# Attention products with 64 rows padded to 128 rows in a one-core transformer layer in fp32

## What is computed

```python
def diff_attention(q, k, v, ...):            # branch A, 4 heads with 2 maps each
    ...
        s = jnp.einsum('bqhmd,bkhmd->bhmqk', q[:, q0:k_len], k[:, :k_len]) * scale
        s = jnp.where(allowed, s + bias[None, :, None], NEG_INF)
        p = jax.nn.softmax(s, axis=-1)
        w = p[:, :, 0] - lam * p[:, :, 1]
        outs.append(jnp.einsum('bhqk,bkhe->bqhe', w, v[:, :k_len]))
...
def sliding_window_sink_attention(...):      # branch B, 8 heads on 2 heads of k and v;
    ...                                      # a chunk of 64 queries sees 2 chunks of 64 keys
def chunk_band_attention(...):               # branch C, 8 heads, all earlier chunks
```

## Time and profile before

| | before |
|---|---|
| median of 3 runs | 924.96 us (924.56 to 925.87) |
| profiled execution, first to last instruction | 925.7 us |
| PE busy | 900.7 us, 97% |
| DVE, ACT, POOL busy | 453.8, 396.4, 369.5 us |
| share of PE in the chain that ended last | 86% |
| attention slots in the trace | from about 39 us to about 353 us |

### The profile page before, as it was taken

One profiled execution on the slowest core, in us unless ns is written; L12 is line 12 of the kernel. 1 busy time (PEld: TensorE's weight loads), 2 busy tenths in 40 slices (PEclk: granted clock), 3 DMA queues, 4 the chain that ended last, 5 costly groups with the idle time before them and its releaser, 6 DMA issues.

```text
span 925.7 us, 12765 instructions
## 1 busy us (share of the span) xinstructions
PE 900.7 (97%) x4327; PEld 742.3 (80%) x4327; DVE 453.8 (49%) x887; ACT 396.4 (43%) x700; POOL 369.5 (40%) x195
## 2 busy tenths in 40 slices
PE   7999999999999999999999999999999999999997
PEld 6877777877787778788888779888888888888886
DVE  4677786665566562353334155655555555400004
ACT  4455445566555563434333144534443444312112
POOL 4333223322222332754455454544444444444441
PEclk9999999999999999999999999999999999999999
DMA  7431133221222210433333721433333332323202
GB/s 226 128 112 45 46 90 91 72 73 59 63 63 75 74 58 24 137 101 92 90 92 113 241 77 47 137 91 91 106 97 91 92 107 95 113 102 103 91 23 92
DMA packets 132140, 86.13 MB, mean 93 GB/s; under 512 B 6822, under 2 KB 121454, under 8 KB 132098
## 3 DMA queue, kind: packets, MB, share of 16 engines
q1 hardware_dynamic: 131050, 81.86, 29.5%
q10 hardware_dynamic: 1048, 3.72, 1.2%
HBM read 83.42 MB, written 2.14 MB: 92 GB/s over the span
## 4 chain that ended last, share of the span: by engine, by line
PE 86%; DVE 8%; ACT 2%; issue 2%; DMA 1%; POOL 0%; ACTq 0%; DVEq 0%; SPq 0%; POOLq 0%
PE banks L1220 26%; PE banks L1222 26%; PE banks L1221 26%; PE banks L1363 3%; PE banks L1295 2%; PE banks L1294 2%; DVE lam_ratio L1045 1%; DMA wide<-in_g_pre_mix_dram 1%; PE banks L1239 1%; DVE pages L942 1%; ACT pages L657 1%; DVE scratch L878 1%; DVE pages L937 1%; DVE scratch L1020 1%; ACT pages L623 0%
## 5 line engine op out<-in xcount | busy, mean ns | idle before, releaser
L518 POOL TENSOR_TENSOR ring_lo<-ring_raw,ring_hi 128x1024 fp32r<-128x1024 f32 x142 | 343.8, 2423 | 499.0 <-ACT ring_hi L615 498.8
L1220 PE MATMUL banks<-u_hi,ring_hi 128*128 128x512 f32 (+1 forms) x800 | 310.3, 388 | 0.0
L1222 PE MATMUL banks<-u_hi,ring_lo 128*128 128x512 f32 (+1 forms) x800 | 305.6, 382 | 0.0
L1221 PE MATMUL banks<-u_lo,ring_hi 128*128 128x512 f32 (+1 forms) x800 | 305.1, 381 | 0.0
L615 ACT CAST ring_hi<-ring_raw 128x1024 fp32r<-128x1024 f32 x142 | 147.7, 1043 | 133.4 <-PE banks L1222 125.3
L1222 PEld LDWEIGHTS banks<-u_hi,ring_lo 128*128 128x128 f32 x800 | 150.7, 188 | 29.5
L1220 PEld LDWEIGHTS banks<-u_hi,ring_hi 128*128 128x128 f32 x800 | 151.0, 189 | 27.5 <-DVE u_lo L884 0.2
L1221 PEld LDWEIGHTS banks<-u_lo,ring_hi 128*128 128x128 f32 x800 | 151.0, 189 | 27.5
L1185 DVE SCALAR_TENSOR_TENSOR wide<-banks,cols,wide 128x511 f32<-128x511 f32 x88 | 65.9, 749 | 87.4 <-ACT wide L837 80.6
L1220 PE MATMUL banks<-ring_hi,pages 128*128 128x512 f32 x240 | 93.8, 391 | 1.7 <-DVE scratch L1118 1.6
L1221 PE MATMUL banks<-ring_lo,pages 128*128 128x512 f32 x240 | 93.4, 389 | 0.0
(11 more groups left out here) (134 smaller groups left out, 1051.1 us busy)
## 6 DMA issues: line engine op xcount, KB each, us to landing
ring_raw<-in_w_ffn_up_dram SPq DMA_DIRECT2D x88, 256.0 KB, 3.1
ring_raw<-in_w_in_dram SPq DMA_DIRECT2D x60, 256.0 KB, 3.3
ring_raw<-in_w_gate_dram SPq DMA_DIRECT2D x48, 256.0 KB, 3.1
ring_raw<-in_w_ffn_down_dram SPq DMA_DIRECT2D x44, 256.0 KB, 2.7
ring_raw<-in_w_out_dram SPq DMA_DIRECT2D x16, 256.0 KB, 2.9
scratch<-in_x_dram SPq DMA_DIRECT2D x4, 512.0 KB, 6.5
ring_raw<-in_w_proj_a_dram SPq DMA_DIRECT2D x8, 256.0 KB, 2.7
ring_raw<-in_w_proj_c_dram SPq DMA_DIRECT2D x8, 256.0 KB, 3.0
```

What stands on the lines that cost most here:

```text
L518: pool.tensor_tensor(wlo[:, r, :], raw[:, r, :], whi[:, r, :].bitcast(F32), ALU.subtract).then_inc(w_lo_done, 1)
L1220: pe.matmul(out, lhs_hi, rhs_hi, start=start, stop=False)
L1221: pe.matmul(out, lhs_hi, rhs_lo, start=False, stop=False)
L1222: return pe.matmul(out, lhs_lo, rhs_hi, start=False, stop=stop)
```

## The change

Three places are changed.

The low part of q gets a page for each map (`q_lo_page(u, m)`), in which the rows of the other map are zero, and L1295 reads all 128 rows of q and of k. DVE clears the four half pages at the start of the program, and `qk(0)` waits for it. The number of products stays.

In B the two blocks of keys change places (the whole tile first), and `pv` reads all 128 rows of the half tile's block: the rows 0 to 63 of its probabilities are zero. POOL clears them once, in slot 33, after `pv(31)`; `pv(33)` waits for it.

`turn_probs` takes its columns accordingly. ACT and DVE copy the two blocks in the new order, with the same shapes.

```diff
+Q_LO_PG = Y_HI + 10
...
-    return qt * P - CHUNK, [(qt - 1, CHUNK, CHUNK), (qt, 0, P)]
+    return qt * P - CHUNK, [(qt, 0, P), (qt - 1, CHUNK, CHUNK)]
...
-        def q_lo_page(u):
-            return QK_PG + 5 * (u % 2) + 2
+        def q_lo_page(u, m):
+
+            return QK_PG + 5 * (u % 2) + 2 if m == 0 else Q_LO_PG + u % 2
...
+                if s == TT * 8 + 1:
+
+                    pool.wait_ge(pv_done, TT * 8)
+                    pool.wait_ge(w_lo_done, sum(split_slot(t) <= s for t in range(T_ATT + RING)))
+                    pool.memset(pages[0:CHUNK, PT_PG:PT_PG + 4, P:2 * P].bitcast(F32), 0.0).then_inc(probs_cleared, 1)
+                    pool.wait_ge(probs_cleared, 1)
...
+            dve.memset(pages[CHUNK:P, QK_PG + 2:QK_PG + 8:5, :].bitcast(F32), 0.0).then_inc(q_lo_cleared, 1)
+            dve.memset(pages[0:CHUNK, Q_LO_PG:Q_LO_PG + 2, :].bitcast(F32), 0.0).then_inc(q_lo_cleared, 1)
...
-                            hi, lo = pages[half_rows(m), q_page(n, m), :], pages[half_rows(m), q_lo_page(n), :]
+                            hi, lo = pages[half_rows(m), q_page(n, m), :], pages[half_rows(m), q_lo_page(n, m), :]
...
-                        rows = half_rows(m)
-                        pairs = ((pages[:, q_page(u, m), cq], pages[:, k_page(u, m), ck]),
-                                 (pages[rows, q_lo_page(u), cq], pages[rows, k_page(u, m), ck]))
+                        pairs = [(pages[:, pg, cq], pages[:, k_page(u, m), ck])
+                                 for pg in (q_page(u, m), q_lo_page(u, m))]
...
+                if s == 4 * 8 + 1:
+                    pe.wait_ge(probs_cleared, 1)
-                for b, (kt, p0, nk) in enumerate(blocks):
-                    rows = slice(p0, p0 + nk)
+                for b, (kt, _, _) in enumerate(blocks):
+
                     pc = slice(b * P, (b + 1) * P)
-                    v_hi_b, v_lo_b = (pages[rows, pg, kt * P:(kt + 1) * P] for pg in (vh, vl))
+                    v_hi_b, v_lo_b = (pages[:, pg, kt * P:(kt + 1) * P] for pg in (vh, vl))
...
-                                    v_hi_b, v_lo_b, pages[rows, PT_PG:PT_PG + 2, pc],
-                                    pages[rows, PT_PG + 2:PT_PG + 4, pc], b == 0, b == len(blocks) - 1)
+                                    v_hi_b, v_lo_b, pages[:, PT_PG:PT_PG + 2, pc],
+                                    pages[:, PT_PG + 2:PT_PG + 4, pc], b == 0, b == len(blocks) - 1)
...
-                    col = 0
-                    for b, (_, _, nk) in enumerate(blocks):
+                    for b, (kt, p0, nk) in enumerate(blocks):
+                        col = kt * P + p0 - k0
                         last = pe.transpose(psum[0:nk, PT_BANK + m, b * P:(b + 1) * P],
                                             scratch[:, P_PAGE + m, col:col + nk], ident[:])
-                        col += nk
...
+            pe.wait_ge(q_lo_cleared, 2)
             qk(0)
```

More of the change, by code:

```diff
@@ L297, in build_encoder @@
         mask_b_done = sem("mask_b_done")
+        q_lo_cleared = sem("q_lo_cleared")
+        probs_cleared = sem("probs_cleared")
         squares = sem("squares")
@@ L1328, in pv @@
                     pe.wait_ge(y_lo, y_count(u - 1, qt // 2))
-                for b, (kt, p0, nk) in enumerate(blocks):
-                    rows = slice(p0, p0 + nk)
+                if s == 4 * 8 + 1:
+                    pe.wait_ge(probs_cleared, 1)
+                for b, (kt, _, _) in enumerate(blocks):
                     pc = slice(b * P, (b + 1) * P)
-                    v_hi_b, v_lo_b = (pages[rows, pg, kt * P:(kt + 1) * P] for pg in (vh, vl))
+                    v_hi_b, v_lo_b = (pages[:, pg, kt * P:(kt + 1) * P] for pg in (vh, vl))
                     if branch(u) == "A":
                         last_b = b == len(blocks) - 1
-                        pe.matmul(psum[:, O_BANK + s % 2, 0:2 * P], pages[rows, PT_PG, pc],
-                                  pages[rows, vh:vh + 2, kt * P:(kt + 1) * P], start=b == 0, stop=False)
-                        mm = pe.matmul(psum[:, O_BANK + s % 2, 0:P], pages[rows, PT_PG + 2, pc], v_hi_b,
+                        pe.matmul(psum[:, O_BANK + s % 2, 0:2 * P], pages[:, PT_PG, pc],
+                                  pages[:, vh:vh + 2, kt * P:(kt + 1) * P], start=b == 0, stop=False)
+                        mm = pe.matmul(psum[:, O_BANK + s % 2, 0:P], pages[:, PT_PG + 2, pc], v_hi_b,
                                        start=False, stop=last_b)
@@ L1350, in turn_probs @@
                 u, qt = divmod(s, TT)
-                _, blocks = keys_of(u, qt)
+                k0, blocks = keys_of(u, qt)
                 maps = 1 if branch(u) == "A" else 2
```

## The result

The changed kernel took 914.37 us (median of 4 runs, 911.96 to 915.46) against 925.41 us of the kernel before in the same series (4 runs): a ratio of 0.9872, with a 95% interval of 0.9855 to 0.9889. So it is faster, by 11.0 us. The forecast was 907.3 with a range of 902.5 to 912.5: the direction was right, and the time lies outside the range.

What follows compares the result with a forecast made beforehand. The prediction took PE, busy for 97% of the span, as the bound: 24.9 us saved on PE, 7.2 lost in waits, 17.7 kept. 924.96 - 17.7 = 907.3 us, range 902.5 to 912.5 with half of rivals 1 and 2.

Steps and rivals of the forecast that it cites:

- The price of a passage between 64 and 128 rows: On PE, each passage between 64-row and 128-row products costs about 0.17 us; four score products hold four passages.
- Rivals 3 to 5: PE's clock falls, 931 (2%); change doesn't do what it says, 924 to 926 (1%); 64-row products already overlap, 935 (1%).
- rival 1: PE keeps everything it saves, 24.9 us, because its waits move with it: 899 to 903.5; 8%.
- the first scores: Scores ahead of the loop: 0.5 us kept.
- the slots with qt = 1: Middle slots with scores of 384 keys: 0.68 us saved and kept in each, but 0.33 in slot 1.
- the slots with qt = 0 but slot 4: First slots of units, 256-key scores: nothing kept in 0, 8, 12; 0.46 us in 16; 0.66 each in 20, 24, 28.
- the cover of the clearings: DVE's two clearings at the start, at most about 2.5 us, hide in 8.7 idle us before its load lands; nothing added.
- three signs of being wrong: The qt = 3 stretches change length, middle slots show waits, or more windows stand at half clock.
- The step that failed: Last slots of units (qt = 3): stretch keeps its length, moving with the transposes before; 4.5 us of savings there become waits.
- rival 2: Waits swallow more: DVE steps newly fall beside POOL's, each such slot giving back 0.7 us; 911 to 920; 14%.
- The base: Starting time of the forecast: runs' median of 924.96 us, taken as 0.7 below the profiled execution's span of 925.7.
- The bounds that the prediction names: One clock fall either way, 1.2 us for transposes, 0.6 for POOL, 0.02 on each of 31 savings: 903.5 to 911, 74%.

Runs made afterwards that it cites:

- back_512: The changed kernel with 64 rows again in the 512-key scores of units 1, 2, 3 and 7 alone; 912.5 us in one run.
- own_bank: The changed kernel with branch A's transposes of v and y in the PSUM bank that its probabilities don't use; 916.21 us in one run.
- pool_late: The changed kernel with POOL's low part of the weights waiting for the slot's probabilities in slots with qt = 3; 906.24 us, ratio 0.9776.
- back_pv: The changed kernel with 64 rows of the half tile again in pv(33), pv(37), pv(41) and pv(43), new block order kept; 914.5 us in one run.
- half_only: The changed kernel with only B's half tile at 128 rows and the new block order, A's and C's scores as before; 922.99 us, ratio 0.9969.

## Why the prediction was wrong

**What held.** The price of a passage between 64 and 128 rows did: 0.12 and 0.23 us a step, 0.94 for `pv`, 23.3 us off PE. Rivals 3 to 5 are out, and so is rival 1. So did the first scores, the slots with qt = 1, slots 1 and 2, the slots with qt = 0 but slot 4, the cover of the clearings, and PE's waits for L1069 (5.7 us, "about 5.6") and L1102 (3.1 us, "2 to 3"). The attention's end did not: the transposes of slot 47 start at 345.1 us in place of 358.3, so 13.2 earlier and not 18. Two of the three signs of being wrong that the prediction named did come: the slots with qt = 3 changed length (8.04 to 8.30 us in A), and the middle slots of A showed waits (for L988). With the clock alike the attention and the two `pv` behind it kept 13.6 us; the sum had 17.7.

**The step that failed** is this, under the last slots of a unit: "so the stretch keeps its length. This holds for its slow steps too [...]: POOL's work starts from ACT's, which moves with the same chain." ACT's L626 hangs on the transposes of y in the slots with qt = 2 of units 1 to 3, not on the transposes of the probabilities; POOL's L523 starts from it and holds DVE; and the sums of the pairs stay at 14.96 to 14.99 us whatever PE saves in between (`back_512`, `own_bank`). All of 3 x 0.70 = 2.1 us was counted as kept and was lost. The time of 914.4 lies in the range of rival 2 (a DVE step beside POOL takes back 0.7 us in a slot), and the mechanism is near it, but it was not in the middle slots, where that rival looked for it, and in the slots read hardly a step newly fell beside POOL (in slot 19 L1037 takes 0.27 us in place of 0.17): those that were held before are held on.

**The same mistake, smaller.**
- I had read for slots 6, 10 and 14 only that the softmax is done early, and overlooked that `turn_probs` waits there for the low part of y as well, which the kernel's text says. `own_bank` removed it and got the forecast 6.25. By itself it cost nothing, as the pair was bound anyway. In slot 18 the same wait has no such cover and is most of the 0.2 us lost in 18 + 19: the slot saved 0.57 us and not 0.70, and its transposes start at 163.71, 0.14 us after L988's end.
- Slot 31 grew from 8.31 to 8.99 us: 0.7 us lost. DVE waits 0.90 us for ACT's L710, which stands behind L681 (k of B) in ACT's queue; L960 follows late, and PE's scores wait for it:

```profile
248.89 0.33 PE L1306 MATMUL banks<-pages 128*128 128x128 f32 x1 [0.50 <-DVE pages L960]
```

  From L681's start to slot 31's transposes it takes 8.94 us in after and in before (241.06 to 250.00, and 251.85 to 260.79), whatever PE does in between. The pair of slots 30 and 31 keeps its sum too, 15.22 before, 15.18 after and 15.16 in `back_512`. POOL has no part in it: slot 31 takes 8.98 in `pool_late`. Another order of ACT's queue was not tried.
- In B 0.21 us of each `pv` ahead of a last slot, and of slot 44, comes back as a wait (`back_pv`), and the rest saved 0.35 rather than 0.4: 0.9 us in all. Slots 18 + 19 lost 0.2, and 22 + 23 and 26 + 27 together gained 0.2 more than thought.
- Slot 4: its 0.45 was read in the one execution in which the clock fell there; in others there is nothing to save.

2.1 + 0.7 + 0.9 + 0.45 make 4.15 us, and 4.1 lie between 17.7 and 13.6; what is left over are differences of 0.1 to 0.2.

**The base.** "The median of the runs lies 0.7 below that execution" had the span against a time. The execution's time was 927.5, and the kernel's median in four series of 7 to 17 runs is 925.4 to 927.3. Against 926.4 the forecast's base of 925.0 is 1.4 us low. The forecast missed 913.4 by 6.1: 4.1 in the slots, 1.4 in the base, and 0.6 between 13.6 and 13.0, which is within what the clock moves. In the first comparison, at 914.37, the clock of the changed kernel was lower (0.990, 0.991, 0.993 and 0.997 in its four runs); whether its falls are more frequent is open. The bounds that the prediction names add up to 3.5 us down and 4.1 up, so its range would be 903.8 to 911.4 and not 903.5 to 911, which changes nothing.

**Open.** Half-clock stretches of 6.8 us between 21 and 30 us turned up in 6 of the 10 profiles of unfilled kernels with the change or a part of it, and in none of the three of the kernel before and of the order alone. `half_only` has them though its start is that of before, and the mean clock of its 8 runs is that of the 9 of before beside them (0.9955 and 0.9954), so chance is likely, but with three profiles against ten it isn't settled. In five of them the first scores start at 40.3 to 41.2 us, in profiles without them at 38.1 to 39.1.

## What to carry to other kernels

A saving on the busiest engine is kept only between the points from which the next stretch is really released. Look for these points by following the last wait back over every engine, other work's queue entries too, and test whether the two neighbouring stretches keep their sum. An instruction of a few elements that lasts microseconds is held by another engine, and moving that one may be worth more than the change at hand: here one wait on POOL gave 7.2 us on top of the 13 of all the padding. Take the base from times of executions, and at least a dozen of them where the forecast turns on one microsecond.

## What the runs showed of the hardware

- A passage between products of 64 and of 128 rows costs TensorE about 0.17 us each time, whatever the columns (four of them 0.66 us at 256 and 0.67 at 384 and 512), and a little more in `pv` (0.39 for two). Zeros in the spare rows cost nothing: a step of 256 columns takes 0.12 us with them.
- Some DVE instructions that take 0.2 to 0.9 us by themselves, one on 128 x 1 numbers among them, lasted up to 2.5 us when POOL's 2.4 us TENSOR_TENSOR had begun first. In after L1037 and L1058 ended with it within 0.02 us, and L1062 on 128 x 128 (slot 12) 0.14 us behind it. The price is thus not a factor but the rest of POOL's instruction. Others, as L1033 (0.69 us), ran beside it at their usual length.
- PE's clock fell to 1.2 GHz for 3.4 us, in places for 6.8, after some of PE's waits of 1 to 2 us and not after others of the same length, in slots that change from execution to execution; a fall of 3.4 us in a slot cost 1.0 to 1.6 us.
